# Input projection of a hybrid pooling and chunked-attention block: eight half-size block products become seven

## The reference

```python
h = rms_norm(x, norm_gain)
proj = einsum('bsd,de->bse', h, w_in)        # 1024 -> 3072: pool_v, pool_g, q, k, v, attn_g, 512 each
y_pool = multiscale_pool(pool_v, pool_w, pool_scale) * silu(pool_g)   # 4 groups of 128, windows 2, 4, 8, 16
y_attn = chunked_rel_attention(q, k, v, rel_bias) * silu(attn_g)      # 8 heads of 64
x = x + einsum('bse,ed->bsd', concatenate([y_pool, y_attn]), w_out)
return rms_norm(x, final_norm_gain)
```

## Time and profile before

| what | value |
|---|---|
| runs | 1870.58 us median of three (1869.71 to 1871.69) |
| profiled execution | 1869.13 us, of which the span from first to last instruction is 1867.4 us |
| mean granted clock of TensorE | 0.985 |
| busy share of the span | PE 94%, PEld 59%, DVE 50%, ACT 39%, POOL 26% |
| matmuls | 14,176 |
| DMA | 168.87 MB, mean 90 GB/s |
| chain that ended last | PE 79%, DVE 8%, SP's queue 4%, DMA 3%, ACT 3%, issue 2% |

### The profile page before, as it was taken

The page is one execution under the profiler, slowest core; times in us unless marked ns, Lnnn a source line. Parts: engine busy times, 40 slices in busy tenths (PEclk is TensorE's granted clock), DMA queues, the critical chain, the costliest instruction groups (busy, mean ns, idle before and its releaser), DMA issues.

```text
span 1867.4 us, 35922 instructions
## 1 busy us (share of the span) xinstructions
PE 1755.8 (94%) x14176; PEld 1103.6 (59%) x14176; DVE 934.6 (50%) x2175; ACT 726.4 (39%) x1438; POOL 494.3 (26%) x580
## 2 busy tenths in 40 slices
PE   7799999999999799999999999999999999999986
PEld 5344444444445556666676666766767667666654
DVE  6555554465441236455364553635536355463544
ACT  6322231232110226354362543625436254462643
POOL 1111110111002014143151432514325152241523
PEclk9899999999999899999999999999999999999988
DMA  9435235334515212122211212122122221122101
GB/s 314 143 113 192 91 125 189 131 116 157 169 66 180 76 36 75 49 64 81 59 50 57 64 64 60 66 57 64 52 65 72 58 64 52 58 79 57 64 29 58
DMA packets 142396, 168.87 MB, mean 90 GB/s; under 512 B 7304, under 2 KB 117400, under 8 KB 140200
## 3 DMA queue, kind: packets, MB, share of 16 engines
q1 hardware_dynamic: 141208, 165.50, 27.4%
q0 software_dynamic: 1040, 1.31, 0.4%
HBM read 92.55 MB, written 54.05 MB: 79 GB/s over the span
## 4 chain that ended last, share of the span: by engine, by line
PE 79%; DVE 8%; SPq 4%; DMA 3%; ACT 3%; issue 2%; POOL 0%; POOLq 0%; ACTq 0%
PE bank L859 17%; PE bank L854 16%; PE bank L265 9%; PE bank L245 5%; PE bank L246 5%; PE bank L247 5%; PE bank L880 4%; PE bank L905 4%; PE bank L935 3%; SPq L1358 3%; DVE res L1237 2%; PE bank L960 2%; PE bank L962 2%; DMA kl<-nat 2%; PE bank L961 2%
## 5 line engine op out<-in xcount | busy, mean ns | idle before, releaser
L1311 POOL TENSOR_TENSOR p_l<-p,p_h 128x256 f16<-128x256 f32 (+1 forms) x376 | 383.6, 1023 | 834.0 <-ACT p_h L1087 833.8
L854 PE MATMUL bank<-hT,wa_h 128*128 128x256 f16 x2048 | 351.2, 273 | 1.2 <-DMA hT<-h_split 0.9
L859 PE MATMUL bank<-wa_h,hT 128*128 128x512 f16 x1024 | 319.3, 379 | 0.0
L854 PE MATMUL bank<-hT,wa_l 128*128 128x256 f16 x1024 | 280.0, 273 | 0.0
L1082 ACT ACTIVATE p<-bank 128x256 f32<-128x256 f32 (+1 forms) x376 | 190.2, 506 | 148.8 <-DVE bank L1205 145.2
L1188 DVE CUSTOM_DVE_ANT_0 junk<-bank,bias_q 128x640 bf16<-128x640 f32 (+4 forms) x256 | 199.4, 779 | 53.3 <-PE bank L905 53.3
L854 PEld LDWEIGHTS bank<-hT,wa_h 128*128 128x128 f16 x2048 | 198.2, 98 | 32.1 <-DMA hT<-h_split 1.1
L1087 ACT ACTIVATE p_h<-p 128x256 f16<-128x256 f32 (+1 forms) x376 | 204.4, 544 | 11.9
L245 PE MATMUL bank<-hT,wp_h 128*128 128x512 f16 x512 | 195.6, 382 | 1.5 <-DVE hT L451 1.5
L246 PE MATMUL bank<-hT,wp_h 128*128 128x512 f16 x512 | 195.6, 382 | 0.0
L247 PE MATMUL bank<-hT,wp_l 128*128 128x512 f16 x512 | 195.4, 382 | 0.0
(11 more groups left out here) (109 smaller groups left out, 2934.1 us busy)
## 6 DMA issues: line engine op xcount, KB each, us to landing
xin<-in_x SPq DMA_DIRECT2D x32, 512.0 KB, 5.1
xres<-in_x SPq DMA_DIRECT2D x32, 512.0 KB, 3.4
h_split<-hT SPq DMA_DIRECT2D x16, 1024.0 KB, 6.9
residual<-xres SPq DMA_DIRECT2D x32, 512.0 KB, 2.6
hT<-h_split SPq DMA_DIRECT2D x16, 1024.0 KB, 5.1
res<-residual SPq DMA_DIRECT2D x32, 512.0 KB, 4.0
out<-res SPq DMA_DIRECT2D x32, 512.0 KB, 2.7
wst<-in_w_in SPq DMA_DIRECT2D x16, 512.0 KB, 6.8
```

The lines of the kernel that those rows point to most:

```text
L854: mm = nc.tensor.matmul(bank[:, 0:AT], w, hT2[:, 1 if p == 1 else 0, kt, :], start=(m == 0), stop=(m == 23))
L859: mm = nc.tensor.matmul(bank[:, :].rearrange("p (c n) -> p c n", c=4), hT2[:, 1 if p == 2 else 0, kt, i * P:(i + 1) * P], w, start=(m == 0 ...
L1311: nc.gpsimd.tensor_tensor(p_l[:, h % 2, c + a:c + b], p32[:, s, a:b], p_h[:, h % 2, c + a:c + b], ALU.subtract).then_inc(A["pl_done"], 1)
```

## The change

The projection's product is done by blocks of two in positions, in depth and in output columns. Seven block products with sums of operand blocks take the place of eight (Strassen's sums in the form with shared intermediate sums). With a = left blocks (h), b = right blocks (w) the sums are s1 = b21' + b22', s2 = s1 - b11', s3 = b11' - b21', s4 = b12' - s2 for the weights, and four of the same kind for h, and the results are combined from the products with three running sums u.

It is laid out in three stages.

- `h_phase_*`, 16 pairs of 128-position blocks. It makes the seven h operands of each pair (three copies by ACT, four sums by DVE from the transposes, their highs by ACT, lows by DVE or POOL), stores them (`h_dram`, 1.75 MiB a pair), and makes v and the attention gate with h stationary and 512 weight columns moving; results go to memory (`v_dram`, `z_dram`). Four pairs (`FOLD_AT`) also fold a pooling group's weights, split in the pair after it.
- `q_phase_*`, 8 tiles of 512 positions by 4 groups: seven products of 12 matmuls with 256 columns moving per group, pooling and output as before; the k and q weights are split on the side (`wk_*`). At its end the k and q of attention tile 0 (`kq_half`).
- `a_phase_*`: the attention as before, but v and gate are loaded (`load_v`, `load_gate`), and k and q of tile t+1 are made in 28 half products of 12 matmuls with 128 columns, 8 in `boundary` and 20 among the heads (`KQ_SLOTS`). The output product uses the banks of the scores. k's and q's high and low parts are taken at fixed heads, by ACT and POOL. Both moves start after the last scores of the tile before. The second half of w_out is loaded and split in tile 0. All loops are unrolled.

The core of the diff (all phases are rewritten; of the removed lines only those that the text speaks of are shown):

```diff
-VRING = 8
-CHUNKS_LOOPED = 2
+PRODUCTS = 7
+ROLE = (0, 1, 2, 3, 0, 2, 3)
+
+FOLD_AT = (1, 4, 7, 10)
...
+            def product(p, s):
+
+                if p == 0:
+                    pe.wait_ge(H["w_lo"], 2 * s + 2)
...
+                for kt in range(4):
+                    hh = hop1[:, p % 2, s, 0, kt * P:(kt + 1) * P]
+                    hl = hop1[:, p % 2, s, 1, kt * P:(kt + 1) * P]
+                    bank = pj[ROLE[s]]
+                    nc.tensor.matmul(bank[:, :], hh, wvg[:, s, 0, kt, :], start=(kt == 0 and s < 4), stop=False,
+                                     skip_group_check=True)
...
+            for p in range(PAIRS):
+                for s in range(PRODUCTS):
+                    product(p, s)
+                    if p in FOLD_AT:
+                        if s == 0:
+                            fold_transposes(FOLD_AT.index(p))
+                        if s == 2:
+                            transposes(2 * p + 2)
+                            fold_products(FOLD_AT.index(p))
+                        if s == 4:
+                            transposes(2 * p + 3)
+                    elif p + 1 < PAIRS:
+                        if s == (4 if p == 0 else 1):
+                            transposes(2 * p + 2)
+                        if s == (5 if p == 0 else 3):
+                            transposes(2 * p + 3)
...
+            for m in range(GROUPS * PTILES):
+                t, k = m // GROUPS, m % GROUPS
+                for s in range(PRODUCTS):
+                    product(m, s)
+                for b in outputs_after(t, k):
+                    output(t - 1, b)
+            for i in range(14):
+                for half in range(2):
+                    kq_half(pe, 0, 2 * i + half)
+            for b in range(PBLK):
+                output(PTILES - 1, b)
...
+        KQ_PRODUCT = (0, 1, 2, 3, 4, 6, 5)
+        KQ_TAKES = {1: 0, 2: 1, 3: 2, 5: 3, 6: 4}
+
+        KQ_BEFORE = 8
+        KQ_SLOTS = ((2, 1), (2, 1), (2, 1), (2, 1), (2, 1), (2, 1), (1, 1), (0, 0))
+        K_HI_AT, Q_HI_AT = (2, 0), (7, 0)
...
+        def kq_half(pe, t, x):
+
+            w, s, pair = 2 * t + x // 14, x % 14 // 2, x % 2
...
+            for kt in range(4):
+                wh, wl = wkq[:, o, 0, kt, column, :], wkq[:, o, 1, kt, column, :]
+                nc.tensor.matmul(dst, wh, hop3[:, o, 0, kt, :], start=(kt == 0 and s < 2 and pair == 0), stop=False,
+                                 skip_group_check=True)
+                nc.tensor.matmul(dst, wh, hop3[:, o, 1, kt, :], start=False, stop=False, skip_group_check=True)
+                mm = nc.tensor.matmul(dst, wl, hop3[:, o, 0, kt, :], start=False, stop=(kt == 3), skip_group_check=True)
...
+        def kq_hi(act, w):
+            act.wait_ge(A["kq_p"], 2 * w + 2)
+            act.wait_ge(A["kq_u"], 5 * w + 5)
+            at_least(act, A["moved_q" if w % 2 else "moved_k"], 96 * (w // 2))
+            nc.scalar.activation(nat_of(w, 0), cs_flat(), ACT.Copy).then_inc(A["nat_hi"], 1)
+
+        def kq_lo(pool, w):
+            pool.wait_ge(A["nat_hi"], w + 1)
+            nc.gpsimd.tensor_tensor(nat_of(w, 1), cs_flat(), nat_of(w, 0), ALU.subtract).then_inc(A["nat_lo"], 1)
...
+        def move_q(sp, t):
+            sp.wait_ge(A["nat_lo"], 2 * t + 2)
+            if t > 0:
+                sp.wait_ge(A["st_mm"], seq(t - 1, HEADS, 0))
...
+        def move_k(sp, t):
...
+            sp.wait_ge(A["nat_lo"], 2 * t + 1)
+            if t > 0:
+                sp.wait_ge(A["st_mm"], seq(t - 1, HEADS, 0))
...
             def boundary(t):
 
-                part("g", t, 0, 0, 24)
+                if t < LAST:
+                    for x in range(4):
+                        kq_half(pe, t + 1, x)
                 if t > 0:
                     values(t - 1, HEADS - 1)
-                part("g", t, 1, 0, 24)
+                if t < LAST:
+                    for x in range(4, 6):
+                        kq_half(pe, t + 1, x)
                 if t > 0:
                     for j in range(2):
                         branch_transposes(t - 1, j)
-                for i in range(4):
-                    part("k", t, i, 0, 24)
+                if t < LAST:
+                    for x in range(6, KQ_BEFORE):
+                        kq_half(pe, t + 1, x)
...
             def heads(t):
                 for h in range(HEADS):
                     last = len(groups(t)) - 1
-                    fillers = [(kind, t + 1, i, a, b) for kind, i, a, b in fill(h)] if t < LAST else []
-                    for k in range(last):
-                        scores(t, h, k)
+                    for k in range(2):
+                        if k < last:
+                            scores(t, h, k)
                         if h + 1 < HEADS:
                             maxima(t, h + 1, k)
-                        if fillers:
-                            part(*fillers.pop(0))
+                        if t < LAST:
+                            for x in slot(h, k):
+                                kq_half(pe, t + 1, x)
...
             for t in range(ATILES):
+                if t == 0:
+                    for n in range(NKT):
+                        load_wob(n)
+                    sp.wait_ge(A["wob_lo"], NKT)
+                else:
+                    move_k(sp, t)
+                    move_q(sp, t)
+                    load_v(sp, t)
+                    load_gate(sp, t)
...
                 for j in range(2):
                     load_residual(t, j)
+                if t + 2 < ATILES:
+                    for s in range(PRODUCTS):
+                        load_hop3(sp, t + 2, s)
```

More of the change, by code:

```diff
@@ L146, in build @@
[L146 to L174, removed]
@@ new lines, in build, with bank6, role_free @@
+        r_stored = [sem(f"q_r_stored{s}") for s in range(2)]
+        pj6 = psum[0:6]
+        op = [wide[:, 0:512], wide[:, 512:1024]]
+        LASTM = GROUPS * PTILES - 1
+        def bank6(m, role):
+            return pj6[(4 * m + role) % 6]
+        def role_free(eng, m, role):
+            if role == 0:
+                eng.wait_ge(Q["c11_done"], m + 1)
+            else:
+                eng.wait_ge(Q["u_done"], 5 * m + (1, 4, 5)[role - 1])
+        WK_STEPS = 8
+        WK_FIRST = 2 * GROUPS
@@ L485, in pool @@
-                for level in range(g + 1):
-                    dst = win[:, level % 2, :]
-                    lo = 2 * back - 1
-                    dve.wait_ge(S["step_done"], step[0])
-                    link(nc.vector.tensor_tensor(dst[:, lo:], src[:, lo:], src[:, lo - back:HIST + PT - back], ALU.add))
-                    src, back = dst, 2 * back
-                other = win[:, (g + 1) % 2, 0:PT]
-                dve.wait_ge(S["step_done"], step[0])
-                link(nc.vector.scalar_tensor_tensor(
-                    out=other, in0=src[:, HIST:], scalar=1.0 / w, in1=v[:, HIST:], op0=ALU.mult, op1=ALU.subtract))
@@ L568, in p_phase_dve, with wot_lo @@
-            for n in range(2 * GROUPS, STARTUP):
-                split_lo(n)
-            tile(0, before=False)
-            with dve.Fori(0, PTILES - 2) as it:
-                tile(it + 1)
-            tile(PTILES - 1, more=False)
-            dve.wait_ge(S["y_done"], GROUPS * PTILES)
-            dve.nop().then_inc(A["inputs_used"], 1)
+                        op0=ALU.mult, op1=ALU.add).then_inc(Q["r_done"], 1)
+            def wot_lo(n):
+                dve.wait_ge(Q["wot_hi"], n + 1)
+                nc.vector.scalar_tensor_tensor(
+                    out=wot_l[:, n, :], in0=wot_stage(n), scalar=WS, in1=wot_h[:, n, :],
+                    op0=ALU.mult, op1=ALU.subtract).then_inc(Q["wot_lo"], 1)
@@ new lines, in build, with slot, kq_bank @@
+        KQ_PRODUCT = (0, 1, 2, 3, 4, 6, 5)
[3 more added lines that the diff above has]
+        K_HI_AT, Q_HI_AT = (2, 0), (7, 0)
+        def slot(h, i):
+            before = KQ_BEFORE + sum(sum(s) for s in KQ_SLOTS[:h]) + sum(KQ_SLOTS[h][:i])
+            return range(before, before + KQ_SLOTS[h][i])
+        def kq_bank(s):
+            bank = (bankx, banky, bankx, banky, bankx, banky, bankx)[s]
+            at = (0, 0, AT, AT, 0, AT, AT)[s]
+            return bank[:, at:at + AT]
```

1935 lines of the change are left out of this document (1220 added, 715 removed).

## The result

The changed kernel takes 1884.4 us (median of 4 runs, 1883.0 to 1885.7), beside 1870.95 of the kernel before on the same chip: ratio 1.007, 95% interval 1.0057 to 1.0083. The forecast was 1840; faster was given 0.70. The time lies inside the stated range (1790 to 1905), but it rose where a fall was forecast.

A forecast was written before the change was run, and what follows sets the result against it. PE's column pace and, in attention heads, the maxima loop through DVE were taken as bounds. First mark 857.5, tiles 0 and 1 105, thirteen tiles 804.7, last tile 69.5: 1836.7, hence 1840 us; range 1790 to 1905, own range 1815 to 1872.

The forecast's parts named there:

- First pair: Start of the first stage: paced by DVE, 33 us of work from the gain's arrival at 8, ending at 45.5.
- Other pairs: Rest of the first stage: 20.1 us a pair on PE, side engines' work all hidden, four folds 12.2 more, end at 357.
- The seam: From first to second stage: no term in the sum; only the range allowed seams of the two stages up to 20.
- Second stage: 32 steps 293.8 us, 28 outputs 145, waits for banks 8 and for DVE 2; end at 806.
- First k and q: Tile 0's k and q before attention: 336 matmuls and two seams, 20 us.
- Columns: Projection matmuls: columns set PE's pace, 55 ns per 128-wide one; 999 us before, 880 after.
- The rival of weight loads: 128-column projection matmuls: weight loads bind, 118 us more if half hidden, 231 if bare; 1958 us total if half hidden; 2%.
- Heads: Attention tile's seven steps: the maxima loop through DVE binds, removed filler becomes idle time; 38.6 us against 38.8.
- Boundary: From a tile's last mark to the next tile's first: 23.3 us where it was 39.5, moves hidden.
- Tiles 0 and 1: First two attention tiles: fewer columns, same chain, output weight splitting in tile 0; 48 and 57, 105 us for 142.4.
- The clock falls: Attention heads: idle gaps on PE lower the granted clock, a tile's head matmuls lengthen by about 12 us; 1925; 6%.
- The rival on the other side: Attention heads: takes, high and low parts delay the maxima chain, 2.0 to 6 us a tile; 1910 at 5; 17%.

The follow-up runs named there:

- Experiment 5: Changed kernel with the six sums of value and gate weight halves moved from POOL to DVE: 1878.0 us.
- experiment 1: Changed kernel with SP issuing the two bias expansions behind, not ahead of, the second stage's first h operands: 1869.8 us.
- experiment 4: Changed kernel with the next k and q weight load issued right behind the h operands, ahead of the residual blocks' stores and loads: 1872.6 us.
- experiment 3: Changed kernel with both low parts of tile 0's k and q made on POOL ahead of the attention masks: 1875.0 us.
- experiment 6: Changed kernel with a head's three halves reordered around the second maxima, two and one before: three and none 1945.1 us, one and two 1873.5 us.
- the four mends and tile 0 as it was: Changed kernel with bias, low-part, weight-load and weight-sum edits, one half before the second maxima and two behind, except in tile 0: 1832.6 us.
- The last kernel: The four mends and tile 0 as it was, plus the first four outputs split over two steps: 1825.8 us, ratio 0.9762 to the kernel before.

## Why the prediction was wrong

The direction failed on one term of the sum, the time of the first mark: 857.5 forecast, 911.2 measured. What failed are the steps in front of the attention: each side engine's work was priced alone, and what queues and the clock cost was put at nothing or next to it. The 53.7 are 13.6, 4.0, 9.3, 14.6, 9.6 and, for the last outputs and the first maximum, 2.6 (34.0 for 31.4). The steps:

- *First pair, "end at 45.5": wrong by 13.6, though 59.05 is still inside the "40 to 60" given for it.* The sum took DVE's split at its price alone and left out POOL's sums. Side by side DVE's splits and POOL's subtractions each take nearly twice their time, and POOL's chain is itself late. Experiment 5 shows the mechanism, and that it is worth some 5 us. The lower clock, up to 7.1, had no term either. By the Trainium skill ("SBUF — State Buffer", section "SBUF: two separate sides") DVE with two SBUF inputs and GpSimd reading SBUF take turns at a shared pair of ports; the trace agrees: in the 9.6 us from 22.86 to 32.42 ran four splits (4.9 alone) and four subtractions of POOL (4.6 at 1.16), in turns 9.5. That rule spoke against this change, and the prediction did not weigh it.
- *Other pairs, 311.7, "all hidden":* 315.8, over by 4.0; the clock is 1.00, and PE waits 7.6 in five transposes, 6.3 of it for DVE's normalisations.
- *The seam, at nothing: wrong by 9.3, and about 2 more of clock.* The prediction asked what SP moves, not what stands in SP's queue ahead of the first operands (experiment 1).
- *Second stage, 449:* 463.5. The takes' waits are 7.5 where 2 were taken (experiment 4), the outputs' 9.6 where 8 were taken, and the clock had no term: it is at its lower level for 4.6 us behind the seam and 3.4 us behind each of the waits of 3.3 and 3.4, up to 5.7 us lost. These make 12.8 of the 14.6; the rest was not followed.
- *First k and q, 20:* 29.6, one wait of 7.6 and its clock; without them 19.5 (experiment 3).
- *Columns:* right. The 128-wide products start 55 ns apart over whole halves, and 336 of them take 19.5 us with 1.1 of wait in experiment 3:

```profile
847.63 0.22 PE L1459 MATMUL bank<-middle,weights 128*128 128x128 f16 x1
847.68 0.22 PE L1461 MATMUL bank<-middle,weights 128*128 128x128 f16 x1
847.74 0.22 PE L1462 MATMUL bank<-middle,weights 128*128 128x128 f16 x1
```

  The rival of weight loads is out. The Trainium skill's 81 ns at 128 columns ("TensorE: Matmul & The Clock Gate", "Back-to-back issue gap") is not what this trace shows; the measurement decides.
- *Heads, 38.6, "nothing is gained":* 37.8. Right in cause, experiment 6 moves the loop both ways, and nearly in size. *Boundary, 23.3:* 22.8. *Tiles 0 and 1, 48 and 57:* 54.9 and 54.8, so the 4.6 over hide two misses. In tile 0 DVE waits 5.8 for ACT's highs of the output weights and the granted clock is 0.88; which of the two costs the 6.9 no run shows. *Last tile, 69.5:* 69.8.
- *"The clock falls":* not in tiles 2 to 14, 0.99 over them and 1.00 in tile 8's window. It fell where the prediction did not look: in the first pair (0.86), behind the two long waits and the two of 3.3 and 3.4, and in tile 0.

The rival on the other side, a longer chain in the heads, did not happen; slower came from another place. The forecast's "seams of the two stages up to 20" was the bound that should have been wider: four places each had a term of 7 to 14 in front of the attention, all of one sign. That the total is off by 44 and not by 54 is no merit of the sum: tiles 2 to 14 came out 14.2 shorter than forecast, 1.1 a tile.

With the four mends and tile 0 as it was, the first mark (876.2) still lies 18.7 us behind the forecast: 7.2 in the first pair, where matmuls at half rate come to 5.1, 3.5 over the other pairs, 3.4 in the second stage, 5.1 between the end of k and q and the mark, less 0.5 in k and q. The last kernel took 9.2 of it away, most of it in the second stage; the first stage was not tried further and stays open.

## What to carry to other kernels

Where a change lays a new stage in front of a loop, sum its seams queue by queue: for each first operand, what stands ahead of it on the engine that issues or makes it, masks, constants and stores included. Price a side engine's work beside the operations that run with it, not by its row alone. Find a loop's second link before shortening the first: moving work off the chain of the maxima gave 1.1 us a tile of 2.7, while putting work on it cost the whole of it.

## What the runs showed of the hardware

- DVE and POOL slow each other when both read two operands from SBUF: a 128x1024 split takes 1.87 us on average against 1.21, and up to 3.4 beside a 128x1024 sum of POOL; a 128x512 subtraction of POOL takes 2.1 against 1.16, a sum up to 3.3 against 2.3. DVE operations with one operand in PSUM are not slowed (0.68 us beside POOL's subtractions at 54 us in experiment 5's kernel, as alone).
- An expansion of single elements, DRAM to DRAM, held SP's queue 6.7 us (9.9 in experiment 1's kernel), and the next store took 9.7 to issue against 0.3 to 1.3 otherwise.
- A wait of 9.1 us on PE cost some 11 and one of 7.6 about 10: PE comes back at 1.2 GHz and stays there some 5 us. Behind waits of 3.3 and 3.4 us the granted clock was 0.57 over 4 us.
- `tensor_scalar` of 128x2 (the minus) takes from 0.17 to 1.08 us in the same place of different steps. The changed kernel's trace says what makes the difference: of its 128, the 57 that take over 0.25 all began while POOL was in an operation, and ended 24 to 29 ns after that one's end. One of them, DVE and POOL:

```profile
1041.59 1.08 DVE L1874 TENSOR_SCALAR m<-mx 128x2 f16<-128x2 f32 x1
```
```profile
1040.51 2.13 POOL L1508 TENSOR_TENSOR middle<-middle 128x1024 f16<-128x1024 f32 x1
```

  It stands on the loop that sets the step: 0.36 on average between 1000 and 1800 us, against 0.17 where POOL is not in its way. No run moved POOL's work away from it.
